# Constant matmuls ahead of the first products, wider spacing in the gated attention, retention's value GEMM moved ahead of five rotary tiles, and one activation table preloaded

## The reference

```python
def first_block(x, ...):
    n = rms_norm(h, norm1_g)
    proj = n @ w_in                       # 1024 x 6672
    ...
    log_a = log_sigmoid(g_low @ gla_gate_up + gla_gate_bias) / 16
    y_gla = rms_norm(gla_attention(q, k, v, log_a), gla_out_norm_g) * silu(g_out)
    mixed = sigmoid(gate_moba) * (y_moba @ w_branch_moba) + sigmoid(gate_gla) * (y_gla @ w_branch_gla)
    h = h + mixed @ w_out
    return h + square(relu(rms_norm(h, norm2_g) @ w_up)) @ w_down

def hybrid_layer(x, ...):                 # twice
    fq, fk, fv, f_logit, rq, rk, rv, rg = split(x @ w_in)
    fox_out = fox_attention(fq, fk, fv, log_sigmoid(f_logit + b_forget))
    ret = retention_chunkwise(rotary(rq), rotary(rk) * 128 ** -0.5, rv, gamma)
    ret_out = silu(rg) * head_groupnorm(ret, ret_gn_g)
    x = layernorm(alpha * x + concat([fox_out, ret_out]) @ w_out)
    return layernorm(alpha * x + square(relu(x @ w_ff1)) @ w_ff2)
```

## Time and profile before

| | us |
|---|---|
| median of 3 runs | 2123.97 (2123.3 to 2124.76) |
| the profiled execution | 2123.57 |
| its span, first to last instruction | 2121.8 |
| PE busy in it | 2055.1 (97%) |
| DVE busy | 1101.9 (52%) |
| ACT busy | 939.3 (44%) |

### The profile page before, as it was taken

The page is one execution under the profiler, slowest core; times in us unless marked ns, Lnnn a source line. Parts: engine busy times, 40 slices in busy tenths (PEclk is TensorE's granted clock), DMA queues, the critical chain, the costliest instruction groups (busy, mean ns, idle before and its releaser), DMA issues. The chain is left out here.

```text
span 2121.8 us, 24498 instructions
## 1 busy us (share of the span) xinstructions
PE 2055.1 (97%) x9660; PEld 1691.6 (80%) x9660; DVE 1101.9 (52%) x1795; ACT 939.3 (44%) x1513; POOL 149.4 (7%) x207
## 2 busy tenths in 40 slices
PE   8999999999999999999999999999999999999997
PEld 6888778888888888777688888888777688888886
DVE  5655556565343443576486333337676476333336
ACT  5664334335232332565557243244565347243343
POOL 0000000000000000353000000000353000000000
PEclk9999999999999999999999999999999999999999
DMA  7332213333322332632323332330632323333321
GB/s 236 95 105 64 77 60 99 121 98 120 119 91 88 100 99 61 179 100 75 114 80 102 99 103 95 100 99 21 199 91 83 114 80 100 100 99 100 99 80 40
DMA packets 201519, 211.38 MB, mean 100 GB/s; under 512 B 7803, under 2 KB 181115, under 8 KB 201404
## 3 DMA queue, kind: packets, MB, share of 16 engines
q1 hardware_dynamic: 194544, 194.13, 29.2%
q0 software_dynamic: 6352, 15.24, 2.8%
q10 hardware_dynamic: 508, 0.43, 0.1%
HBM read 194.55 MB, written 8.95 MB: 96 GB/s over the span
## 5 line engine op out<-in xcount | busy, mean ns | idle before, releaser
L298 PE MATMUL ps<-Phi,wh 128*128 128x512 f32 (+1 forms) x1208 | 481.1, 398 | 18.9 <-DVE Plo L448 8.7
L301 PE MATMUL ps<-Phi,wl 128*128 128x512 f32 (+1 forms) x1208 | 459.3, 380 | 0.1
L300 PE MATMUL ps<-Plo,wh 128*128 128x512 f32 (+1 forms) x1208 | 458.4, 380 | 0.0
L269 ACT ACTIVATE wh<-stage 128x1024 fp32r<-128x1024 f32 (+2 forms) x253 | 261.5, 1041 | 183.9 <-PE ps L301 167.1
L270 DVE TENSOR_TENSOR wl<-stage,wh 128x1024 fp32r<-128x1024 f32 x250 | 304.6, 1223 | 66.2 <-ACT wh L269 58.5
L298 PEld LDWEIGHTS ps<-Phi,wh 128*128 128x128 f32 x1208 | 228.4, 189 | 67.0 <-issue 19.6
L301 PEld LDWEIGHTS ps<-Phi,wl 128*128 128x128 f32 x1208 | 227.7, 188 | 44.7 <-DVE wl L270 0.8
L300 PEld LDWEIGHTS ps<-Plo,wh 128*128 128x128 f32 x1208 | 228.5, 189 | 40.8 <-issue 4.1
L298 PE MATMUL ps<-Qhi,wh 128*128 128x512 f32 (+1 forms) x680 | 256.2, 377 | 0.8 <-DVE Qlo L445 0.8
L301 PE MATMUL ps<-Qhi,wl 128*128 128x512 f32 (+1 forms) x680 | 254.4, 374 | 0.0
L300 PE MATMUL ps<-Qlo,wh 128*128 128x512 f32 (+1 forms) x680 | 254.4, 374 | 0.0
(11 more groups left out here) (301 smaller groups left out, 2921.5 us busy)
## 6 DMA issues: line engine op xcount, KB each, us to landing
stage<-in_w_ff SPq DMA_DIRECT2D x64, 1024.0 KB, 5.4
stage<-in_w_in SPq DMA_DIRECT2D x39, 1024.0 KB, 5.3
stage<-in_w_up SPq DMA_DIRECT2D x16, 1024.0 KB, 5.3
stage<-in_w_down SPq DMA_DIRECT2D x16, 1024.0 KB, 5.2
stage<-in_w_in SPq DMA_DIRECT2D x30, 512.0 KB, 5.3
stage<-in_w_out SPq DMA_DIRECT2D x12, 1024.0 KB, 5.2
stage<-in_w_bg SPq DMA_DIRECT2D x4, 1024.0 KB, 5.4
vrev<-H SPq DMA_DIRECT2D x2, 2048.0 KB, 14.9
```

What stands on the lines that cost most here:

```text
L269: t_hi = A.op(lambda e: e.activation(hi, src, ACT.Copy), st_landed[n, part], w_free[u], sem=s_whi)
L298: PE.op(lambda e: e.matmul(o, hi[:, k, c], x.hi[:, kx, tok], start=first, stop=False), t_hi, t_x or x.t[kx], list(waits), signal=False)
L300: PE.op(lambda e: e.matmul(o, hi[:, k, c], x.lo[:, kx, tok], start=False, stop=False), signal=False)
L301: return PE.op(lambda e: e.matmul(o, lo[:, k, c], x.hi[:, kx, tok], start=False, stop=last), t_lo, sem=s_wpe, signal=last)
```

## The change

There are five edits.

1. **Start.** DVE fills `rB` with ones, and PE runs four matmuls of 512 columns of f32 on it into bank 7, ahead of the first product. Nothing reads what they make. The squares and their sums come three tiles after the splits, so that three tiles are split before the first is squared.
2. **GLA.** The first head's scores come two steps later after its gates, each head's average one step later after the sum of squares, and the pace rises from 0.52 to 0.55.
3. **Table.** ACT loads the table of natural logarithm and exponential once, after the sigmoids of the first block. In the built order 12 of 18 table loads go (the two of `rms_scale`, two at the first hybrid layer's attention, eight in its retention), and one comes.
4. **Value GEMM.** It, and its weights in the load order, stand ahead of rotary tiles 3 to 7. Its outputs 1 to 3 are centred by chores. `retention` is put in the background before tiles 3 to 7 and waits for the rotary tiles that it needs; outside the softmax chores are emitted at once (`put_off`, `turns`).
5. `gemm` asks `settled(b)` for its bank, as `gemm_tok` did.

```diff
@@ -204,8 +204,8 @@
             pair_cols(w_in2[L], 2)
             cols(w_in2[L], 1672, 1928)
             pair_cols(w_in2[L], 3)
+            values(w_in2[L], 2568, 3080)
             cols(w_in2[L], 1928, 2568)
-            values(w_in2[L], 2568, 3080)
             cols(w_in2[L], 3080, 3592)
             cols(w_out2[L], 0, 1024)
             for g in range(4):
@@ -214,7 +214,7 @@
 
         st_landed, st_free = {}, [None, None]
         w_tok, w_free, slot = {}, [None] * 7, {}
-        state = {"slab": 0, "prep": 0, "use": 0, "bank": 0, "ahead": 3}
+        state = {"slab": 0, "prep": 0, "use": 0, "bank": 0, "ahead": 3, "turns": False}
         ring_free = [0, 1, 2, 3]
 
         def load_slab():
@@ -315,7 +315,7 @@
                 b = next_bank()
                 o = banks[b][0:m, :]
                 for k in range(nk):
-                    t = product(o, w, k, slice(c0, c0 + m), x, k, k == 0, k == nk - 1, free[b] if k == 0 else None)
+                    t = product(o, w, k, slice(c0, c0 + m), x, k, k == 0, k == nk - 1, settled(b) if k == 0 else None)
                     tick()
                 free[b] = evac(o, t)
             x.free = t
@@ -388,6 +388,12 @@
             if chores:
                 chores.pop(0)()
 
+        def put_off(*what):
+
+            chores.extend(what)
+            while chores and not state["turns"]:
+                chore()
+
         def settled(b):
 
             while chores and free[b] == [OWED]:
@@ -465,6 +471,7 @@
         c1 = V.op(lambda e: e.memset(ones[:, :], 1.0))
         c2 = V.op(lambda e: e.memset(onec[:, :], 1.0 / 1024))
         c3 = V.op(lambda e: e.memset(onev[:, :], 1.0 / 256))
+        idle = V.op(lambda e: e.memset(rB[:, :], 1.0))
         c4 = V.op(lambda e: e.memset(epsc, 1e-6))
         c5 = V.op(lambda e: e.memset(eps5, 1e-5))
         t_cst = A.op(lambda e: e.dma_start(cst[:, :], consts[:, 0:256]), sem=s_c[5], inc=16)
@@ -485,11 +492,18 @@
         lhs = at("t5col", g0 + 72, [33, 128])
         t5 = bass.AP(tensor=prm[:, :].tensor, offset=V_T5, ap=[[V_END, 33], [1, 8], [0, 16]])
         t_l = V.op(lambda e: e.tensor_copy(lhs[:, :].rearrange("p (h c) -> p h c", h=8), t5), t_prm)
+        for _ in range(4):
+            t_idle = PE.op(lambda e: e.matmul(banks[7][:, :], ones[:, :], rB[:, :], start=True, stop=True), idle, c1)
+        free[7] = rb_free[0] = t_idle
         t_acc = None
-        for k in range(8):
-            split(P, k, H[:, k, :], [t_x[k // 2], t_prm], prm[:, V_G1 + k:V_G1 + k + 1])
+        for k in range(11):
+            if k < 8:
+                split(P, k, H[:, k, :], [t_x[k // 2], t_prm], prm[:, V_G1 + k:V_G1 + k + 1])
             if k == 0:
                 prepare()
+            k -= 3
+            if k < 0:
+                continue
             t_s = A.op(lambda e, k=k: e.activation(sq[k % 2][:, :], H[:, k, :], ACT.Square), t_x[k // 2], sq_free[k % 2])
             if k == 0:
                 t_acc = V.op(lambda e: e.tensor_copy(accq[:, :], sq[0][:, :]), t_s, done(PE))
@@ -509,7 +523,7 @@
                         t_acc, free[4], t_const)
             t = A.op(lambda e: e.activation(tB[:, :], banks[4][:, :], ACT.Ln, bias=epsc), t_m, rb_free[0], t_const)
             free[4] = t
-            t = A.op(lambda e: e.activation(rB[:, :], tB[:, :], ACT.Exp, scale=-0.5), t, rb_use)
+            t = A.op(lambda e: e.activation(rB[:, :], tB[:, :], ACT.Exp, scale=-0.5), t, rb_use, t_idle)
             rb_free[0] = t
             t_rB[:] = [t]
 
@@ -735,6 +749,7 @@
                     free[7] = finished(h, o, t)
                 owed.append(end)
 
+            state["turns"] = True
             bias_for(0)
             bias_for(1)
             for n in range(-3, 32):
@@ -764,6 +779,7 @@
             while chores:
                 chore()
                 yield
+            state["turns"] = False
 
         def split_values(vv, b, o, t, sc, *waits):
 
@@ -918,7 +934,7 @@
                 yield
             for _ in gates(0):
                 yield
-            for _ in range(3):
+            for _ in range(5):
                 yield
             for hd in range(4):
                 qd = gqk[:, hd, :]
@@ -989,6 +1005,7 @@
                 sq_free[1] = t
                 yield
                 yield
+                yield
                 tp = PE.op(lambda e: e.matmul(banks[5][:, :], onev[:, :], sq[0][:, :], start=True,
                                               stop=True), t, free[5], t_const)
                 t = A.op(lambda e: e.activation(tB[:, :], banks[5][:, :], ACT.Ln, bias=epsc), tp, rb_free[0])
@@ -1004,7 +1021,7 @@
                 yield
 
         background.append(gla())
-        pace[0] = 0.52
+        pace[0] = 0.55
         t_go, t_gm = [None] * 8, [None] * 8
         for j in range(8):
             def ev(o, t, j=j):
@@ -1059,6 +1076,7 @@
         for _ in range(4):
             gemm(Q, 4, ev_bm)
         finish_background()
+        A.op(lambda e: e.preload_act_table_set("natural_log_exp_and_others"), signal=False)
         for j in range(8):
             def ev(o, t, j=j):
                 t1 = V.op(lambda e: e.tensor_tensor(gh[:, j, :], o, gh[:, j, :], ALU.mult), t, t_gg[j])
@@ -1498,22 +1516,33 @@
                             op0=ALU.mult, op1=ALU.mult), r_free[0])
                         t_r[j] = r_free[0] = V.op(lambda e: e.tensor_tensor(rdst(j), rdst(j), rb[:, :], ALU.add), t12, t3)
                         box[0] = t3
-                    chores.extend((first_half, second_half))
+                    put_off(first_half, second_half)
                     return box
                 return ev
 
-            for ev in (ev_r(0), ev_fq(2), ev_fk(2), ev_r(1), ev_r(2), ev_fq(3), ev_fk(3),
-                       ev_r(3), ev_r(4), ev_r(5), ev_r(6), ev_r(7)):
+            for ev in (ev_r(0), ev_fq(2), ev_fk(2), ev_r(1), ev_r(2), ev_fq(3), ev_fk(3)):
                 gemm(P, 8, ev)
             t_rv = [None] * 4
 
             def ev_rv(b, o, t):
+                box = [OWED]
+
+                def centre():
+                    box[0] = centred(b, o, t)
+                if b:
+                    put_off(centre)
+                else:
+                    centre()
+                return box
+
+            def centred(b, o, t):
                 t1 = V.op(lambda e: e.tensor_reduce(sums[:, b, :], o.rearrange("p (h d) -> p h d", h=4), AX.X, ALU.add), t)
                 total = bass.AP(tensor=sums[:, :, :].tensor, offset=4 * b, ap=[[16, 128], [1, 4], [0, 128]])
                 t_rv[b] = V.op(lambda e: e.scalar_tensor_tensor(
                     out=rv[:, b, :].rearrange("p (h d) -> p h d", h=4), in0=total, scalar=-1.0 / 128,
                     in1=o.rearrange("p (h d) -> p h d", h=4), op0=ALU.mult, op1=ALU.add), t1, Q.free)
                 return t_rv[b]
+            gemm_tok(P, ev_rv)
             t_fox, t_dec = [], [t_dec0]
 
             def attention_over():
@@ -1541,6 +1570,8 @@
                 it_free, norm = t_fox, iter(())
                 for h in range(4):
                     t_it = []
+                    while t_r[4 + h] is None:
+                        yield
                     for j in range(4):
                         w = S - 128 * j
                         b = 4 + j % 2
@@ -1573,7 +1604,8 @@
                     yield
 
             background.append(retention())
-            gemm_tok(P, ev_rv)
+            for j in range(3, 8):
+                gemm(P, 8, ev_r(j))
             while not t_fox:
                 step_background()
             pace[0] = 0.58
```

## The result

The changed kernel takes 2104.77 us (median of four, 2103.48 to 2106.88) where the kernel before took 2123.64 on the same chip: 0.9912 of it, with an interval of 0.9896 to 0.9928. It is 18.9 us faster; I had said 13.3.

The account below looks back on a forecast made before the run. PE, busy 97% of the span, was taken as the bound, so only its waits counted. Start 0.4, GLA 4.3, tables 0 and value GEMM less retention's loss 8.6 summed to 13.3 us: 2110.5 us, range 2106 to 2116.

Parts of the forecast that it names:

- The start: Kernel start: tile 1 at 12.6 us, then a clock fall giving back 1.6 of 2.0; gain 0.4 us, bounds 0 and 2.0.
- the two rules: Clock at the start: activity releases the throttle, giving 2.0 us; against it, a wait between bursts brings the low clock back.
- the clock holds: Rival: PE keeps the high clock through the start and retention's wait; 15.9 us gained, so 2108; chance 0.17.
- GLA: GLA's waits for kiv and sums of squares: 2.0 and 2.3 us go; gain 4.3 us, bounds 3.3 and 4.7.
- The value GEMM: Value GEMM at its new place: 5.1 us of waits and 1.67 of low clock go in each layer, 6.8 us.
- the softmax turns: Attention's softmax turns: no gain entered; their seven waits, 3.8 us in all, appeared only under a rival that the kernel gets slower.
- Tables: ACT's table loads, eight of 1.28 us each in the first retention: they lie beside PE's work, worth 0.
- Retention: Head of retention: later rotary pieces and decay tables, a 3.3 us wait and a clock fall; loss 2.5 us a layer.
- The value GEMM waited for no bank: Rival that the wait moves along: owed banks or rotary tile 3 bring back 5.1 us a layer; 2119.3, chance 0.11.
- no turn waited longer than before: Rival that the kernel gets slower: DVE bounds the attention's last heads and softmax turns wait for sums; 2129, chance 0.02.

## Why the prediction was off, point by point

**The start: mechanism right, but not certain.** I forecast matmuls of the high clock before 12.6, then a fall and tile 1 at 12.6. The changed kernel's PE there, counterpart of the earlier trace rows:

```profile
1.87 5.77 PE L496 MATMUL ps<-rB,ones 128*128 128x512 f32 x8 [1.87 <-DVE rcol L476]
...
8.50 0.47 PE L298 MATMUL ps<-Phi,wh 128*128 128x512 f32 x1 [0.87 <-DVE Plo L454]
...
10.93 0.50 PE L298 MATMUL ps<-Phi,wh 128*128 128x512 f32 x1 [1.50 <-ACT wh L269]
...
13.02 0.77 PE L298 MATMUL ps<-Phi,wh 128*128 128x512 f32 x1 [0.25 <-DVE Plo L454]
...
24.18 0.59 PE L522 MATMUL ps<-accq,onec 128*128 128x512 f32 x1
```

Tile 1 came 0.4 late, since the second piece came 0.28 late and `wl` with it, and the fall followed: +0.1. But with the same start the clock held in three of six profiles (those with the fraction put back, without the table load, and with retention rearranged), and the norm's matmul then came near 22.4. So the low end of my bounds occurs, and the high one nearly (1.7 of 2.0); one trace of the kernel before could not choose between them. The six profiles part at the constant matmuls, which took 5.4 to 6.7 us. Where the clock fell later, they ended at 7.3 to 7.9 and PE then waited 0.7 to 1.2 us for the first product; where it held, they ended at 8.3 to 8.6 and it waited 0.4 or less. That this wait is the cause is not shown, since no run changed it alone. Of the two rules that I had set against each other from the Trainium skill ("TensorE: Matmul & The Clock Gate", "What's actually happening" and "HAM oscillation — how this bites in real kernels"), the first fits the three profiles in which the constant matmuls were enough, the second the three in which the clock fell again behind the waits that followed them. The rival "the clock holds" is as good a description of the start as my forecast.

**GLA: 4.3 forecast, 5.4 measured.** I let 0.4 of `kiv`'s wait stand, and it went. The other 0.65 is a matter of reading: a wait's row counts from the end of the last matmul, 0.39 us after its start, while matmuls in a row start every 0.227. So each wait that goes is worth its row plus 0.16. 4.7 + 4 x 0.16 = 5.3. The value GEMM says the same: 5.1 + 2 x 0.16 + 1.67 = 7.1, measured 7.1 and 7.2. At the head of retention it does not show: with GLA's edit alone 1.25 us of rows a layer went there, and 1.3 were gained.

**The step that failed: the softmax turns.** I costed GLA's edit by GLA's waits and entered nothing for the attention, naming its seven waits of 3.8 us only as a risk. The changed pace shifts the counter's fraction that the attention inherits, and 3.1 us went up to the value GEMM, the largest part of a miss of 5.5. The times agree that the term was too small: GLA's edit alone gave 7.0 us, at least 5.1 by its interval, where my bounds ended at 4.7. By the fraction put back, 1.7 of the 3.1 reach the end in this kernel; the other 1.4 come back at the head of retention, so the stages are not independent. The wait for `x_IT` is not the whole reason for that: with the rearranged head, which has no such wait, 1.1 came back there all the same.

**Tables: 0 forecast.** Nearly true in the kernel before (0.6 us in its trace). In the changed kernel they are worth 1.0 by the trace, which the times cannot tell: the softmax steps come earlier there, and the first bias, which stands behind ACT's loads, comes too late for them. The term was taken from waits of a schedule that the same change moves.

**Retention: the right list, a clock that held.** In times of the attention's last weighing my forecast put `x_IT` at 8.3 us and PE's second pair of head 1 at 20.5, or 21.0 with the fall that I took; they came at 8.2 and 20.8:

```profile
999.05 0.69 DVE L451 TENSOR_TENSOR Qlo<-x_yf,Qhi 128x512 fp32r<-128x512 f32 x1 [0.70 <-ACT Qhi L450]
...
1003.87 1.15 DVE L1581 TENSOR_TENSOR x_IT<-ps,accq 128x512 f32<-128x512 f32 x2
...
1015.72 1.16 DVE L1581 TENSOR_TENSOR x_IT<-ps,x_dec 128x512 f32<-128x512 f32 x2 [9.04 <-DMA x_dec<-in_consts]
```

The wait of 3.3 is there to 0.02 us. I took a fall of the clock behind it, since an equal wait had one, and lost 0.5 us a layer in the sum. Even a fall would not have cost that: in the three cases where it came (constant matmuls in the waits, no table load) the head took 0.1 to 0.3 us less than here. 0.65 us more a layer came from the norm behind retention. PE's waits of the kernel before have this row for it, which I had not read, and the changed kernel has none:

```profile
PE ps L1530 <- ACT x_wk L1529: 1.3, 2, 0.7
```

In the kernel before this wait, too, hangs on the fraction: the row stands in the runs of the start, the value GEMM and the table alone, and is gone in the three with the fraction at 0.68. In the changed kernel it did not return with 0.84, so there something else holds it off as well. Without a fall the sum was 2.0; 2.3 - 0.65 = 1.65 is what the waits' rows give, and 1.6 and 1.3 were measured.

**The last norm** lost 1.0 us to where the clock fell (1733.2 to 1736.6, before 1739.9 to 1743.3). No edit stands there.

**The rivals.** "The clock holds", 2108, was nearest; it was true for retention in the profiled execution, not for its start, and alone is still 3 us short. The value GEMM waited for no bank, and no turn waited longer than before.

## What to carry to other kernels

A background scheduler that carries a fraction from stage to stage couples stages that share nothing else: where a pace changes, compare the whole order of the following stages, not the edited one alone. A wait at a join gives back what an earlier stage gains, so free the join first: here the rearranged head of retention made the median 12.4 us shorter, 9.5 of it at the two heads by the trace, and the reading that pointed at it was the one wait that the change had made longer. Add to each removed PE wait inside a row of GEMM matmuls the part of the last matmul that the next would have covered (0.16 us here).

## What the runs showed of the hardware that I had not expected

The same instructions with the same wait are followed by a fall of the clock in one execution and not in another. PE's wait of 3.3 us at retention's head occurs twice in each of four profiles (the changed kernel, the value GEMM alone, the constant matmuls in the waits, no table load): the clock fell within a microsecond of its end in three of eight cases, each time for 3.4 us at half. GLA's wait of 2.4 us, which the earlier trace rows showed without a fall, had one in two of six profiles. The stall of the value GEMM (1.8 and 3.3 us with 0.2 us of work between) had one in twelve of twelve, and in five of them the clock stood low for longer: twice 3.4 us in four, 10.2 us at a stretch in one. At the first layer's last norm, which no edit touches, it fell in five of the fourteen profiles and took about 1.5 us each time. So one trace tells what a wait can cost, not what it costs each time; a removed wait is worth its length and its share of falls, and a fall costs nothing where the slower matmuls fill a wait that stands behind it. The mean granted clock over a run shows the same: 0.993 to 0.996 in the four runs of the changed kernel, 0.997 in all five of the rearranged one.

What remains open: how much of the changed kernel's 18.9 us is the fraction and the table load in a mean over executions. The traces give 1.7 and 1.0 with the rest in place; their differences in time, 0.9 and 1.1 us against a median from another chip, lie within what the runs scatter. The edits one by one add up to 15.0 us in time (0.8, 7.0, 7.1 and 0.1), 3.8 less than together; with intervals of 2 to 3 us to either side of a term this is not told from the whole.
